# Cached keys of the samples turned by VectorE in squares of 32x32 instead of by TensorE

## The chip, the core and the metric

The kernel runs on one core of one Trainium2 chip. The time is the device time of one execution in microseconds; the kernel before takes 1926.86 us, the median of three runs (1926.57 to 1928.02).

## What is computed

One step of a layer of a streaming encoder, for a prompt (1024 frames) and for 8 samples of 16 new frames each, with shared weights and float32 throughout. The parts that the change touches, for the samples:

```python
k_all = concat([cache_fox_k, k], axis=1)      # 512 cached + 16 new rows, 8 heads x 64
s = einsum('bqhd,bkhd->bhqk', q, k_all) * 64 ** -0.5 + cq - ck    # branch A, causal
p = softmax(s); o = einsum('bhqk,bkhd->bqhd', p, v_all)
s = einsum('bqhd,bmhd->bhqm', qm, cache_mem_k) * 128 ** -0.5      # branch C, 256 rows, 4 heads x 128
```

Around it lie the input projection, the same attentions for the prompt, a pooling branch, gates and an output projection, and a feed-forward layer with 4096 inner channels.

## The kernel before

Every float32 product is made of parts: an operand is split into a high part (rounded to the fast format by a ScalarE copy) and a low part (the rest, by a VectorE subtraction), and TensorE multiplies high by high, high by low and low by high (`COMBOS`). A weight is so loaded by SP (`load_weights`, L570), its high part made on ScalarE (`split_hi`, L579) and its low part on VectorE (`split_lo`, L597), two buffers deep.

The order of the work is written out by hand. `plan` is the list of projection steps (weights of 128 columns over the tokens in blocks of 384); `product` (L1654) runs half a block, 12 matmuls of 128x384 (in `br` steps, with half the weights, a whole block). The attentions are cut into pieces, and the dictionary `beside` (built by `put`) says in front of which half block each piece is issued; every engine walks the same list and issues its own share of each piece, then the step's own evictions (`leave`) and, at a step's first half, the split of the next weight. So the pieces of the samples stand between half blocks of products on TensorE, in order on each engine.

Branch A's samples are worked in the halves of the steps `qm` and the first `gate` of branch 1, branch C's samples later beside `gate` and `br` steps of branch 1. Each sample i has three pieces, `sample(k, 3 * i + part)`:

- part 0: TensorE multiplies the queries, laid out in `qpad` with zeros for the other heads, by the turned keys `kt`, four quarters of 128 channels one after the other, each waiting for its `kt_lo` (`scores`, L1407); then the values of sample i - 1 (`values`, L1424, L1430). VectorE adds the bias and takes the maximum (L2512), ScalarE exponentiates and scales (L1913, L1923), VectorE copies the output of i - 1 (L2483).
- part 1: TensorE turns the probabilities (`turn`, L1454) and the output of i - 1 (`turned_out`, L1441), then turns quarters 0 and 1 of the keys of i + 1 (`turn_keys`, L1374) into two PSUM banks. ScalarE makes the high parts of the probabilities, of these keys (`keys_hi`, L1882), of the values of i (L1943). VectorE makes the low parts of the probabilities (L2538, L2541) and of the keys (`keys_lo`, L2438), and copies the queries of i + 1 into `qpad` (`queries`, L2452).
- part 2: TensorE turns quarters 2 and 3 of the keys; ScalarE and VectorE make their parts, VectorE then the low part of the values (L2559, in two halves for branch A).

SP issues all loads in the same order: keys of i + 2 in part 2 (part 1 for branch C) once the keys of i + 1 are turned (`load_keys`, L815), then values, bias and the weights. Branch A has one key buffer behind the first sample's own (`kraw_first`, loaded in `fox`, L835), branch C two. `first` is the piece that prepares sample 0: keys, cleared `qpad`, queries. The new queries and keys of the samples (`QS`, `KS`) are written at the eviction of the projections q and k (`leave`), high part by ScalarE, low part by VectorE; GpSimd copies a sample's new keys behind its cached ones (L1133). GpSimd and VectorE also share the new rows' values (L1143 to L1147 on GpSimd). `refill` brings back the prompt's outputs (L2567) in the same halves.

## Time and profile before

| | |
|---|---|
| three runs | 1926.57, 1926.86, 1928.02 us |
| profiled execution, first to last instruction | 1926.4 us |
| its own time beside the span | not given apart; the runs' median is 0.5 us above the span |
| TensorE busy, weight loads busy | 1903.4 us (99%), 1869.4 us (97%) |
| VectorE, ScalarE, GpSimd busy | 1222.8, 842.7, 516.6 us |
| mean granted TensorE clock | 0.999 |
| branch A's samples, branch C's samples | about 545 to 660 us, 777 to 855 us |

Busy time of TensorE counts overlapping matmuls once; a matmul's duration there is longer than the distance between two starts, so costs on TensorE are read from starts.

### The profile page before, as it was taken

The page shows a single profiled execution, that of the slowest core. Times are in us where ns is not written, and L with a number is a line of the kernel's source. Part 1 is how long each engine was busy: PE and PEld are TensorE (multiplying, and loading weights), DVE is VectorE, ACT ScalarE, POOL GpSimd, SP SyncE. Part 2 cuts the span into 40 slices and gives each one's busy share as a digit, 9 for nine tenths or more (in the row PEclk, how much of TensorE's full clock was granted, in tenths as well). Part 3 has the DMA queues.
Part 4 walks back from the last instruction along what each step waited for, and adds up shares of the span by engine and source line. Part 5 has one row for each costly group of instructions (what it writes and reads, how often), then busy time and mean ns, then how long its engine had stood idle before and what let it go on. Part 6 is the DMA issues. An engine that isn't in the chain of part 4 may idle for free. (4 is left out here: it accounts for less than half of the span.)

```text
span 1926.4 us, 33099 instructions
## 1 busy us (share of the span) xinstructions
PE 1903.4 (99%) x12655; PEld 1869.4 (97%) x12655; DVE 1222.8 (63%) x2293; ACT 842.7 (44%) x1672; POOL 516.6 (27%) x547
## 2 busy tenths in 40 slices
PE   9999999999999999999999999999999999999998
PEld 8999999999999999999999999999999999999997
DVE  6685545454557666554334467687777977777765
ACT  7454434353546544443223332344444544444445
POOL 1004324250612123000000004276544433333320
PEclk9999999999999999999999999999999999999999
DMA  6451312213266643444233222233333433333323
GB/s 197 114 134 50 94 47 66 83 35 94 55 231 206 203 137 99 146 154 131 64 104 93 70 88 72 94 100 91 122 89 92 123 91 88 88 88 88 89 93 99
DMA packets 243601, 202.40 MB, mean 105 GB/s; under 512 B 16750, under 2 KB 217966, under 8 KB 243317
## 3 DMA queue, kind: packets, MB, share of 16 engines
q1 hardware_dynamic: 243445, 200.29, 34.8%
q8 instruction: 101, 1.65, 0.4%
q14 instruction: 55, 0.45, 0.1%
HBM read 166.62 MB, written 33.64 MB: 104 GB/s over the span
## 5 line engine op out<-in xcount | busy, mean ns | idle before, releaser
L1654 PE MATMUL ps<-act_hi,w_hi 128*128 128x384 f32 x1128 | 386.9, 343 | 0.9 <-DVE w_lo L597 0.6
L1654 PE MATMUL ps<-act_hi,w_lo 128*128 128x384 f32 x1128 | 378.0, 335 | 0.0
L1654 PE MATMUL ps<-act_lo,w_hi 128*128 128x384 f32 x1128 | 377.6, 335 | 0.0
L597 DVE TENSOR_TENSOR w_lo<-w_raw,w_hi 128x512 fp32r<-128x512 f32 (+1 forms) x200 | 198.0, 990 | 122.3 <-ACT w_hi L579 121.7
L1638 PE MATMUL ps<-ffs_hi,w_hi 128*128 128x288 f32 x832 | 245.8, 295 | 1.0 <-DVE h L2646 0.6
L1638 PE MATMUL ps<-ffs_hi,w_lo 128*128 128x288 f32 x832 | 245.2, 295 | 0.0
L1638 PE MATMUL ps<-ffs_lo,w_hi 128*128 128x288 f32 x832 | 244.9, 294 | 0.0
L1623 PE MATMUL ps<-bp_hi,pw_hi 128*128 128x288 f32 x784 | 231.6, 295 | 0.2 <-DVE pw_lo L2601 0.2
L1623 PE MATMUL ps<-bp_lo,pw_hi 128*128 128x288 f32 x784 | 231.3, 295 | 0.0
L1623 PE MATMUL ps<-bp_hi,pw_lo 128*128 128x288 f32 x784 | 231.2, 295 | 0.0
L579 ACT ACTIVATE w_hi<-w_raw 128x512 fp32r<-128x512 f32 (+1 forms) x200 | 152.6, 763 | 164.5 <-PE ps L1638 119.4
L1654 PEld LDWEIGHTS ps<-act_hi,w_hi 128*128 128x128 f32 x1128 | 212.2, 188 | 2.0 <-DVE w_lo L597 0.9
L1654 PEld LDWEIGHTS ps<-act_lo,w_hi 128*128 128x128 f32 x1128 | 212.2, 188 | 0.4
L1654 PEld LDWEIGHTS ps<-act_hi,w_lo 128*128 128x128 f32 x1128 | 211.7, 188 | 0.0
L1638 PEld LDWEIGHTS ps<-ffs_hi,w_hi 128*128 128x128 f32 x832 | 156.1, 188 | 2.1 <-DVE h L2646 1.4
L1638 PEld LDWEIGHTS ps<-ffs_hi,w_lo 128*128 128x128 f32 x832 | 156.1, 188 | 0.0
L1638 PEld LDWEIGHTS ps<-ffs_lo,w_hi 128*128 128x128 f32 x832 | 156.1, 188 | 0.0
L1623 PEld LDWEIGHTS ps<-bp_hi,pw_hi 128*128 128x128 f32 x784 | 147.0, 187 | 0.9 <-DVE pw_lo L2601 0.8
L1623 PEld LDWEIGHTS ps<-bp_hi,pw_lo 128*128 128x128 f32 x784 | 147.5, 188 | 0.0
L1623 PEld LDWEIGHTS ps<-bp_lo,pw_hi 128*128 128x128 f32 x784 | 147.2, 188 | 0.0
L1170 POOL TENSOR_TENSOR quad<-quad 128x576 f32<-128x576 f32 x16 | 26.3, 1654 | 412.5 <-DVE bp_lo L2595 412.3
L1117 POOL TENSOR_SCALAR fox_p<-fox_p,small 128x128 f32<-128x128 f32 (+7 forms) x64 | 110.6, 1728 | 92.9 <-DVE small L2359 91.3
(356 smaller groups left out, 4190.7 us busy)
## 6 DMA issues: line engine op xcount, KB each, us to landing
w_raw<-in_w_down_dram SPq DMA_DIRECT2D x112, 256.0 KB, 3.4
pair_raw<-in_w_up_dram SPq DMA_DIRECT2D x28, 1024.0 KB, 5.5
w_raw<-in_w_in_dram SPq DMA_DIRECT2D x44, 512.0 KB, 4.4
merged<-prod SPq DMA_DIRECT2D x48, 192.0 KB, 2.0
prev<-merged SPq DMA_DIRECT2D x48, 192.0 KB, 3.8
foxs_vraw<-in_cache_fox_v_dram SPq DMA_DIRECT2D x8, 1024.0 KB, 6.1
foxs_kraw<-in_cache_fox_k_dram SPq DMA_DIRECT2D x7, 1024.0 KB, 5.6
x_in<-in_x_prompt_dram SPq DMA_DIRECT2D x8, 512.0 KB, 4.5
```

Of the source, the lines that this page charges most:

```text
L579: nc.scalar.activation(W[c % 2][0][:, 0:kt, :], w_raw[c % 2][:, 0:kt, :], ACT.Copy).then_inc(w_hi, 1)
L597: nc.vector.tensor_tensor(W[c % 2][1][:, 0:kt, :], w_raw[c % 2][:, 0:kt, :], W[c % 2][0][:, 0:kt, :].bitcast(F32), ALU.subtract).then_inc( ...
L1117: nc.gpsimd.tensor_scalar(p, p, col(RC, u), None, ALU.mult).then_inc(at_s["p_ready"], 1)
L1170: last = nc.gpsimd.tensor_tensor(out, a, b, op)
L1623: last = nc.tensor.matmul(p_bank(q), PW[q % 4][a][:, t, :], BP[PART_ORDER[0].index(i)][z][:, t, :], start=(t == 0 and n == 0), stop=(t == ...
L1638: last = nc.tensor.matmul(bank(b)[:, 0:TQ], W[c % 2][a][:, t, :], FS[k % 2][z][:, t, TQ * h:TQ * (h + 1)], start=(t == 0 and m == 0), stop ...
L1654: last = nc.tensor.matmul(bank(b)[:, 0:width], W[k][a][:, t, :], moving[z][:, t, j * width:(j + 1) * width], start=(t == 0 and n == 0), st ...
```

## The change

The cached keys are no longer turned by TensorE. They are loaded so that VectorE's transpose, which turns each square of 32 partitions by 32 columns where it stands, gives the turned keys: rows of 32 keys go to 32 partitions, and each quarter of the 512 columns to its own group of 32 partitions, by four DMAs with runs of 128 columns (512 bytes) in place of one with runs of 512 (2 KB). Partition 32y + a of quarter j then holds channel 128y + 32j + a, and the queries are laid out alike, by copies of 32 partitions. Turned keys lie in a new buffer `kt_raw` in SBUF, from which ScalarE and VectorE take the two parts.

```diff
+            def send_keys(a, i):
+                for y in range(4):
+                    sp.dma_start(raw_keys(a, i)[quadrant(y), :, :], a.kd[i][:, :, y * P:(y + 1) * P]).then_inc(sa["k_in"], 16)
-                sp.dma_start(raw_keys(a, i)[:], a.kd[i]).then_inc(sa["k_in"], 16)
+                send_keys(a, i)
...
-                sp.dma_start(mqs_raw[:], mem_q[:, :, SEQ:T]).then_inc(me["in"], 16)
+                for h in range(MH):
+                    sp.dma_start(mqs_raw[quadrant(h), :, :],
+                                 mem_q[:, h, SEQ:T].rearrange("(j r) q -> r j q", r=QUAD)).then_inc(me["in"], 16)
...
+            reached(pool, "new_lo", 2)
...
-            def turn_keys(a, i, part):
...
-                    for t in range(a.tiles):
-                        last = nc.tensor.transpose(ps[:, j % 2, t * P:(t + 1) * P], raw[:, t, j * P:(j + 1) * P], ident[:])
-                    last.then_inc(sa["kt_over"], 1)
...
-                    if i + 1 < NB:
-                        turn_keys(a, i + 1, 0)
-                elif i + 1 < NB:
-                    turn_keys(a, i + 1, 1)
...
-                    nc.scalar.activation(a.b["kt"][0][:, j, 0:a.tiles * P], ps[:, j % 2, 0:a.tiles * P],
+                    nc.scalar.activation(a.b["kt"][0][:, j, 0:a.tiles * P], a.b["kt_raw"][:, j, 0:a.tiles * P],
...
+                    if args == (0, 0):
+                        for part, raw in ((QS, qs_raw), (KS, ks_raw)):
+                            nc.scalar.activation(part[0][:], raw[:], ACT.Copy).then_inc(st["new_hi"].sem, 1)
...
-                        last = nc.scalar.activation(rest[0][:, s.i, :], src[:, LAST:TB], ACT.Copy, scale=scale)
+                        for y in range(4):
+                            last = nc.scalar.activation(rest[quadrant(s.i), y, :], src[quadrant(y), LAST:TB],
+                                                        ACT.Copy, scale=scale)
...
+            def keys_turned(a, i, part):
+                c = a.base + i
+                if part == 0:
+                    dve.wait_ge(sa["k_in"], 64 * (c + 1))
+                    if i:
+                        dve.wait_ge(sa["s_over"], c)
+                for j in (2 * part, 2 * part + 1):
+                    nc.vector.transpose(a.b["kt_raw"][:, j, 0:a.tiles * P],
+                                        raw_keys(a, i)[:, :, quadrant(j)]).then_inc(sa["kt_over"], 1)
...
-                    nc.vector.tensor_tensor(a.b["kt"][1][:, j, 0:a.tiles * P], ps[:, j % 2, 0:a.tiles * P],
+                    nc.vector.tensor_tensor(a.b["kt"][1][:, j, 0:a.tiles * P], a.b["kt_raw"][:, j, 0:a.tiles * P],
...
             def queries(a, i):
...
                 for x in range(2):
-                    w = P + NQ * per
-                    z, side = (x, 0) if a.new else (0, P // 2 * x)
-                    for h in range(per):
-                        r = slice(P // per * h, P // per * (h + 1))
-                        dst = a.b["qpad"][z][r, :].rearrange("p (j w) -> p j w", w=w)[:, :, side + h * NQ:side + (h + 1) * NQ]
-                        last = nc.vector.tensor_copy(dst, a.q[x][r, :, i * NQ:(i + 1) * NQ].bitcast(F32))
+                    for y in range(4):
+                        at_ = a.b["qpad"][x if a.new else 0][quadrant(y), :]
+                        new = a.q[x][quadrant(y), :, i * NQ:(i + 1) * NQ].bitcast(F32)
...
+                    keys_turned(a, 0, 0)
+                    keys_turned(a, 0, 1)
                     keys_lo(a, 0, 0)
+                    if a.new:
+                        for n, (part, raw) in enumerate(((QS, qs_raw), (KS, ks_raw))):
+                            reached(dve, "new_hi", n + 1)
+                            nc.vector.tensor_tensor(part[1][:], raw[:], part[0][:].bitcast(F32),
+                                                    ALU.subtract).then_inc(st["new_lo"].sem, 1)
...
                 elif part == 1:
+                    if i + 1 < NB:
+                        keys_turned(a, i + 1, 0)
                     dve.wait_ge(sa["pt_hi"], c + 1)
...
                 elif part == 2:
+                    if i + 1 < NB:
+                        keys_turned(a, i + 1, 1)
                     if i and a.new and i + 1 < NB:
                         out_lo()
-                    if i + 1 < NB:
-                        keys_lo(a, i + 1, 1)
                     dve.wait_ge(sa["v_hi"], c + 1)
...
                     for g in range(pieces):
...
+                        if g == 0 and i + 1 < NB:
+                            keys_lo(a, i + 1, 1)
...
-                    if j == 2:
-                        last = nc.vector.scalar_tensor_tensor(out=rest[1][:, s.i, :], in0=src[:, LAST:TB], scalar=scale,
```

`quadrant(y)` is the slice of partitions 32y to 32y + 31. `load_keys` waits as before for `kt_over`, which VectorE's transposes now count up.

## Rows read from the trace of the kernel before

**Rows 1.** The page: busy time, share of the span, instructions.

```profile
PE 1903.4 (99%) x12655; PEld 1869.4 (97%) x12655; DVE 1222.8 (63%) x2293; ACT 842.7 (44%) x1672; POOL 516.6 (27%) x547
```

**Rows 2.** Stretches: length, busy of PE, PEld, DVE, ACT, POOL, PEclk, DMA, GB/s.

```profile
557.65:572.55 14.90, 14.06 (x99) 13.43 (x100) 8.30 (x19) 7.42 (x14) 1.58 (x3) 1.00 0.87 302
601.19:615.28 14.09, 14.09 (x105) 13.95 (x104) 11.26 (x24) 8.72 (x17) 2.99 (x5) 1.00 0.71 227
...
795.66:805.57 9.91, 9.91 (x64) 9.38 (x63) 4.66 (x15) 5.03 (x13) 0.00 (x0) 1.00 0.43 151
815.60:825.40 9.80, 9.80 (x63) 9.27 (x63) 7.28 (x21) 4.67 (x12) 0.00 (x0) 1.00 0.76 223
```

**Rows 3.** Line L1374, the key turns: ns min/median/max, first and last start.

```profile
L1374 PE MATMUL ps<-ident,foxs_kraw x112: 272/272/331, 559.0 to 648.3; 128*128 128x128 f32 x112
...
L1374 PE MATMUL ps<-ident,mems_kraw x64: 270/272/328, 777.5 to 848.9; 128*128 128x128 f32 x64
```

**Rows 4.** Timeline of PE around the first group: start, length, instruction.

```profile
545.00 0.34 PE L1654 MATMUL ps<-act_hi,w_lo 128*128 128x384 f32 x1
545.18 1.03 PE L1374 MATMUL ps<-ident,foxs_kraw_first 128*128 128x128 f32 x8
545.97 0.42 PE L1654 MATMUL ps<-act_hi,w_hi 128*128 128x384 f32 x1
546.23 0.34 PE L1654 MATMUL ps<-act_lo,w_hi 128*128 128x384 f32 x1
```

**Rows 5.** Timeline of PE, one cycle of branch A.

```profile
601.19 0.60 PE L1454 MATMUL ps<-ident,foxs_p 128*128 128x128 f32 x4
...
608.14 0.40 PE L1407 MATMUL ps<-foxs_kt_hi,foxs_qpad_hi 128*128 128x264 f32 x2
...
611.05 0.64 PE L1424 MATMUL ps<-foxs_v_hi,foxs_pt 128*128 128x256 f32 x4
...
615.28 0.60 PE L1454 MATMUL ps<-ident,foxs_p 128*128 128x128 f32 x4
```

**Rows 6.** Timeline of DVE, the same cycle.

```profile
601.39 1.23 DVE L597 TENSOR_TENSOR w_lo<-w_raw,w_hi 128x1024 fp32r<-128x1024 f32 x1 [1.15 <-ACT w_hi L579]
602.99 0.69 DVE L2538 TENSOR_TENSOR foxs_pt<-ps,foxs_pt 128x512 fp32r<-128x512 f32 x1 [0.37 <-ACT foxs_pt L1932]
...
604.19 1.29 DVE L2438 TENSOR_TENSOR foxs_kt_lo<-ps,foxs_kt_hi 128x512 fp32r<-128x512 f32 x2
...
605.87 0.39 DVE L2452 CAST foxs_qpad_hi<-qs_hi 64x64 fp32r<-64x64 f32 x2
...
606.70 0.23 DVE L2488 TENSOR_TENSOR branch_lo<-o_part,branch_hi 128x64 fp32r<-128x64 f32 x1
607.75 1.29 DVE L2438 TENSOR_TENSOR foxs_kt_lo<-ps,foxs_kt_hi 128x512 fp32r<-128x512 f32 x2 [0.82 <-ACT foxs_kt_hi L1882]
608.95 2.35 DVE L2559 TENSOR_TENSOR foxs_v_lo<-foxs_vraw,foxs_v_hi 128x1024 fp32r<-128x1024 f32 x2
```

**Rows 7.** Timeline of ACT, the weight's high part in that cycle.

```profile
600.32 1.04 ACT L579 ACTIVATE w_hi<-w_raw 128x1024 fp32r<-128x1024 f32 x1
```

**Rows 8.** Timeline of DVE in branch C, the copies of the queries.

```profile
798.11 0.18 DVE L2452 CAST mems_qpad_hi<-mqs_hi 128x64 fp32r<-128x64 f32 x1
798.21 0.19 DVE L2452 CAST mems_qpad_hi<-mqs_lo 128x64 fp32r<-128x64 f32 x1
```

**Rows 9.** The first key load on SP's queue; DMA issues: KB each, us to landing.

```profile
539.26 0.43 SPq L835 DMA_DIRECT2D foxs_kraw_first<-in_cache_fox_k_dram  x1
...
w_raw<-in_w_in_dram SPq DMA_DIRECT2D x44, 512.0 KB, 4.4
...
foxs_kraw<-in_cache_fox_k_dram SPq DMA_DIRECT2D x7, 1024.0 KB, 5.6
```

**Rows 10.** Timeline of PE: first scores of branch A and of branch C.

```profile
551.67 0.51 PE L1407 MATMUL ps<-foxs_kt_hi,foxs_qpad_hi 128*128 128x264 f32 x2 [0.39 <-DVE foxs_qpad_lo L2452]
...
782.56 0.28 PE L1407 MATMUL ps<-mems_kt_hi,mems_qpad_hi 128*128 128x256 f32 x1
```

More of the change, by code:

```diff
@@ L68, in encoder_program @@
     V_LO = 32
+    QUAD = 32
     NTOK = 5
@@ L398, in encoder_program @@
         MQS = parts("mqs", [P, BT, P], R_AT + 65536)
-        sm = dict(kraw=[tensor(f"mems_kraw{k}", [P, MT, 512], R_AT + 36864 * k) for k in range(2)], vraw=tensor("mems_vraw", [P, MT, 512], R_AT + 4096),
-                  kt=parts("mems_kt", [P, 4, MT * P], R_AT + 8192), v=parts("mems_v", [P, MT, 512], R_AT + 16384),
+        sm = dict(kraw=[tensor(f"mems_kraw{k}", [P, NMEM // QUAD, P], R_AT + 36864 * k) for k in range(2)], vraw=tensor("mems_vraw", [P, MT, 512], R_AT + 4096),
+                  kt=parts("mems_kt", [P, 4, MT * P], R_AT + 8192), kt_raw=tensor("mems_kt_raw", [P, 4, MT * P], R_AT + 8192 + 16 * MT * P), v=parts("mems_v", [P, MT, 512], R_AT + 16384),
                   p=tensor("mems_p", [P, MT * P], R_AT + 24576),
@@ L405, in encoder_program @@
                   os=tensor("mems_os", [P, 4, P], R_AT + 69632),
-                  qpad=parts("mems_qpad", [P, 4 * (P + NQ)], R_AT + 31744))
+                  qpad=parts("mems_qpad", [P, 4 * P], R_AT + 31744))
         gate1 = tensor("gate1", [P, T], R3_AT + 1536)
@@ L834, in fox @@
                     sp.wait_ge(at_s["s_over"], UNITS)
-                    sp.dma_start(raw_keys(samples[0], 0)[:], samples[0].kd[0]).then_inc(sa["k_in"], 16)
+                    send_keys(samples[0], 0)
                 if s == 18:
@@ L1359, in fox @@
                     turn(s - 2)
-            def turn_keys(a, i, part):
-                c = a.base + i
-                if part == 0:
-                    pe.wait_ge(sa["k_in"], 16 * (c + 1))
-                    if i == 0 and a.new:
-                        pe.wait_ge(at_s["s_read"], UNITS)
-                    elif i == 0:
-                        pe.wait_ge(at_s["exp"], UNITS + M_UNITS)
-                for j in (2 * part, 2 * part + 1):
-                    if 4 * c + j >= 2:
-                        pe.wait_ge(sa["kt_lo"], 4 * c + j - 1)
-                    raw = raw_keys(a, i)
-                    for t in range(a.tiles):
-                        last = nc.tensor.transpose(ps[:, j % 2, t * P:(t + 1) * P], raw[:, t, j * P:(j + 1) * P], ident[:])
-                    last.then_inc(sa["kt_over"], 1)
             def sample(k, s):
@@ L1547, in beside_pe @@
                     fox(*args)
-                elif what == "first":
-                    turn_keys(samples[args[0]], 0, args[1])
                 elif what == "sample":
@@ L2128, in leave @@
                 elif s.kind in ("q", "k"):
-                    dst, rest, scale = (fq, QS, FD ** -0.5) if s.kind == "q" else (fk, KS, 1.0)
+                    dst, rest, scale = (fq, qs_raw, FD ** -0.5) if s.kind == "q" else (fk, ks_raw, 1.0)
                     if s.i == 0 and s.kind == "q" and j == 0:
@@ L2442, in queries @@
             def queries(a, i):
-                c, per = a.base + i, a.heads // 4
+                c = a.base + i
                 if i:
```

31 lines of the change are left out of this document (21 added, 10 removed).

## The prediction

> **What bounds the kernel now.** I read the page first: TensorE is busy for 99% of the span [rows 1], so the first guess is that work taken from it is time won. Then the table of stretches, one row per cached sample: two cycles of branch A (forgetting attention over 512 cached keys, 8 samples) and two of branch C (256 memory keys, 8 samples). TensorE has no idle time in the middle cycles, and VectorE is busy for 11.26 of 14.09 us in the first kind, 7.28 of 9.80 us in the busiest of the second [rows 2]. So TensorE bounds both stages, but VectorE has only about 2.5 to 3 us per sample left, and this change puts work exactly there. All of it lies in 545 to 660 and 777 to 855 us; the rest of the span keeps its time.
>
> **What it removes.** TensorE turns 16 blocks of keys per sample in A (128 in all, 112 of them in the first row) and 8 per sample in C (64) [rows 3]. Their 272 ns are pipelined times. What they cost is read from the order of starts: products start 0.18 us apart (545.00, 545.18); a group of eight starts at 545.18, the products behind it at 545.97 and 546.23, so the group costs 546.23 - 545.18 - 0.17 = 0.88 us [rows 4]. 16 groups of eight in A are 14.1 us, 16 groups of four in C at half that 7.1 us: 21 us is the most that the removal can give.
>
> **What it adds, per sample of A.** Four VectorE turns of 128x512 from SBUF to SBUF. No row shows such an instruction. The nearest are the 128x512 subtractions: 1.29 us for two in a row [rows 6]. I take 1.29 us for a pair. Lower bound: nothing (a gain from it has no reason); upper: twice that, 2.6 us a pair, if four-byte squares go at half the rate. Second, the copies of the queries become eight of 32 partitions instead of four of 64. The 64x64 copies take 0.39 us for two that start 0.20 us apart [rows 6], the 128x64 copies of C start 0.10 us apart though each takes as long [rows 8]. Copies that change their partitions do not overlap. So I take 0.20 us each: 1.6 us instead of 0.8 in A, 1.6 instead of 0.2 in C; if they did overlap, 0.8 in both. The Trainium skill ("VectorE: DVE Perf Modes", section on two Vector instructions with no wait between them) says that an instruction is held until all earlier ones have finished when its start quadrant of 32 partitions differs from the last one's; all eight copies would be held, and the trace agrees. Had I read the 128x64 row alone, the sum below would be 10 us lower, and the rule gives the other reading. Subtractions and high parts now read SBUF instead of PSUM: 1.29 us for two against half of 2.35 us for two of twice the width [rows 6], no difference.
>
> **The path of one cycle of A.** Take the cycle that begins when TensorE starts to turn the probabilities at 601.19. Before: turns, key turns, a product, key turns, a product, scores at 608.14, values at 611.05, a product, next cycle at 615.28, 14.09 us [rows 5]. The scores take 2.91 us, so the third quarter of the keys is read 1.46 us in, at 609.6; VectorE's low part of it, the first of the pair at 607.75, is ready at 608.4 [rows 6]: 1.2 us of slack, and that is why TensorE never waits.
> After: the pair of turns for quarters 1 and 2 stands ahead of the subtraction at 602.99 and falls into VectorE's idle time. Then as before up to 605.87; copies to 607.5; turns of quarters 3 and 4 to 608.8; the output's low part (0.25) 609.05; the first half of the value's low part, now moved ahead (half of 2.35 us), 610.2; low part of quarter 3 at 610.85, of quarter 4 at 611.45 [rows 6]. TensorE, rid of both groups, is at the scores at 608.14 - 1.76 = 606.4, waits for the queries until 607.5, reaches quarter 3 at 609.0 and waits until 610.85. Then 1.46 for two quarters and 4.23 for values and product [rows 5]: 616.5 against 615.28, +1.25 us. What VectorE has still to do between the low part of quarter 4 and the next probabilities is what it had, and stays within the 5 us that TensorE needs from there. Six cycles: +7.5 us.
> In three of these VectorE also has a weight's low part (1.23 us, after ScalarE's high part of 1.04 us [rows 6, 7]). Today both lie in the gap before 602.99. In the new order the turns stand behind them: 1.04 + 1.15 + 1.29 = 3.5 us after the cycle's start instead of 1.8, some +1.55 each: +4.65 us.
> The cycle from the first to the second sample took 14.90 us [rows 2], for waits of its own; by the same path, without the output parts (0.7), it takes 14.6: -0.3.
> **The first sample.** The keys were issued at 539.26 [rows 9]; four issues end some 1.3 us later, so the last part lands at about 546.2 (5.6 us [rows 9]). From there VectorE: four turns 2.5, two subtractions 1.25, two new ones for the new queries and keys 1.25, two clears, reckoned like subtractions, 1.2, two subtractions 1.25, copies 1.6: 555.3, where the scores started at 551.67 [rows 10]: +3.6 us. TensorE's saved 1.76 us are inside it.
> **Sum for A:** 3.6 - 0.3 + 7.5 + 4.65 = +15.45 us.
>
> **C.** Turns are half as wide (0.32 us each), keys are double buffered. At the start four turns (1.3) and longer copies (1.4) come ahead of the scores that started at 782.56 [rows 10]; I put some 1.6 of these 2.7 us into VectorE's waits: +1.1. In cycles like 815.60 to 825.40 VectorE has 7.28 + 1.3 + 1.2 = 9.8 us of work in 9.8 [rows 2], the gate products' evictions stand in its path, and each gets some 0.6 longer (three of seven); in quiet ones like 795.66 (4.66 busy [rows 2]) TensorE waits 0.6 us of the 0.88 saved plus what it waited for anyway, -0.4 (two); two stay as they are. Sum +2.1 us.
>
> **Parts costed at nothing.** In the projections ScalarE gets three more small copies in eight evictions and VectorE loses one: the bank is needed again two blocks of 4.2 us later; without that cover some 0.8 us each, 6 us. Four key loads instead of one are three issues of 0.4 us more on SP, ahead of values and weights that are asked for a cycle before use. The four loads of the memory queries lie before branch C. GpSimd's new wait is for parts made well before its copies of the new keys, behind which only its value copies queue.
>
> **Total:** 15.45 + 2.1 = +17.6 us on the profiled execution's 1926.4 us of span: 1944.0 us. The three runs' median, 1926.86 us, stands 0.5 us above that span; I leave this within the rounding. 0.2%, about what a measurement tells from no change, is 3.9 us. The bounds of my own case: copies that overlap take 0.8 from each of 15 cycles (-10); turns at 1 us more a pair add some 12: 1934 to 1956.
>
> **Rivals.**
> *VectorE swallows it and TensorE's saving shows (faster).* For it: 99% [rows 1], and that the first pair of turns lies in idle time. Against: the 1.2 us of slack in quarter 3's path. If turns cost nothing and copies start 0.10 apart, quarter 3 is ready at 608.75 and the cycle ends at 614.45: -0.85 in six, -1.8 in the first cycle, +0.3 at the start, -6.5 in C: -13, 1913 us. It decides only where a pair of turns takes under about 0.4 us; with copies 0.20 apart even free turns give no more than 1923.
> *Squares at half rate.* Another 1.29 us for each pair: six cycles +7.2, weights' cycles +3.6, start and first cycle +3.6, C +6: 1964 us. For it: nothing in the trace; against: every row's time goes with its elements.
> *The keys come late.* The load of sample i+2 now waits for VectorE's turns (608.8) instead of TensorE's (606), and its turns are wanted by 617.0 at the latest: 8.2 us, against 5.6 for rows of 2 KB and 4.4 for half the bytes in rows of 512 B [rows 9], so between 5.6 and 8.8. Twice 4.4 costs 0.6 a cycle. If it is 10.5 us: 2.3 in six cycles and 3.6 at the start, +17: 1961 us. The Trainium skill ("SBUF — State Buffer", section Door 1) has a rule against this part of the change: a transfer to 32 partitions reaches 8 of 16 ports, 189 GB/s instead of 328 at 1 MiB; by it the load takes an estimated 2.3 us more, 7.9, and nothing is lost. No run here shows such a load yet.
>
> **How the numbers follow.** Forecast 0.68 (of it 0.08 within 0.2% of before, if copies overlap and turns are at 0.4 us), faster 0.12 (the rows' slack speaks against it, but I never saw a turn), half rate 0.09, late keys 0.11. The range 1923 to 1962 leaves out nearly the whole of the faster case and half of the half-rate one, under 2 in 10. Faster 0.12, same 0.08, slower 0.80.
>
> **What would show it.** Right: no turns on TensorE, A's cycles of 15 to 17 us, TensorE waiting within the scores for the low key parts and for the query copies, turns of 0.6 to 0.7 us, copies 0.20 apart. Wrong: A's cycles at 12.4 us and no waits before the scores, turns of 0.3 us; or long waits of VectorE for the key load, or turns over 1 us.

## The result and the profile after

The changed kernel takes 1965.78 us (median of four runs, 1963.82 to 1968.43) against 1927.0 us (1926.57 to 1928.02) for the kernel before: ratio 1.0201, interval [1.0189, 1.0214]. Forecast were 1944 us and a range to 1962. The profiled execution has a span of 1961.9 us, 35.5 more than before's 1926.4; the forecast for that span was +17.6. Below, the table of stretches is read against spans, and runs against medians.

The page of the changed kernel, first part, answers to [rows 1]: TensorE 5.0 us less, VectorE 47.2 us more.

```profile
PE 1898.4 (97%) x12463; PEld 1862.4 (95%) x12463; DVE 1270.0 (65%) x2431; ACT 853.6 (44%) x1698; POOL 520.3 (27%) x547
```

The table of stretches of the changed kernel (length, busy of PE, PEld, DVE, ACT, POOL, PEclk, DMA, GB/s): up to the first sample's turn, the first cycle, the third, the last; it answers to [rows 2].

```profile
540.00:564.24 24.24, 17.27 (x94) 16.60 (x92) 14.09 (x34) 7.06 (x14) 3.32 (x7) 0.86 0.86 215
564.24:580.75 16.51, 12.66 (x83) 11.80 (x83) 10.64 (x26) 7.51 (x14) 0.00 (x0) 1.00 0.94 233
601.28:620.38 19.10, 14.89 (x88) 14.56 (x87) 14.63 (x32) 10.34 (x18) 3.71 (x5) 0.82 0.64 161
674.92:692.00 17.08, 14.06 (x89) 13.71 (x88) 11.88 (x29) 8.84 (x17) 3.66 (x5) 0.90 0.34 102
```

A cycle here is the time from one sample's first turn of probabilities to the next sample's. Cycles of branch A take 16.5 to 20.5 us instead of 14.1 to 14.9, and the granted clock, 1.00 throughout before, is 0.82 to 0.90 in six of the seven. By places: the first turn of probabilities stands at 564.24 instead of 557.65 (+6.6), the last at 692.00 instead of 657.66 (+34.3), the first scores of C at 815.85 instead of 782.56 (+33.3), the end at +35.5. So nearly all of the loss is in A.

TensorE's timeline in the third cycle of the changed kernel answers to [rows 5] (those rows are of the fourth cycle; there the changed kernel waits 3.28 us before the scores and takes 17.34 us in all). The scores wait 4.21 us, for the previous output's low part (`branch_lo`), and then start 0.44 us apart, two at a time, where they started 0.24 apart before (last two lines, kernel before).

```profile
610.80 0.78 PE L1406 MATMUL ps<-foxs_kt_hi,foxs_qpad_hi 128*128 128x264 f32 x2 [4.21 <-DVE branch_lo L2507]
611.38 0.64 PE L1406 MATMUL ps<-foxs_kt_lo,foxs_qpad_hi 128*128 128x264 f32 x2
611.82 0.64 PE L1406 MATMUL ps<-foxs_kt_hi,foxs_qpad_lo 128*128 128x264 f32 x2
```

```profile
608.38 0.40 PE L1407 MATMUL ps<-foxs_kt_lo,foxs_qpad_hi 128*128 128x264 f32 x2
608.62 0.40 PE L1407 MATMUL ps<-foxs_kt_hi,foxs_qpad_lo 128*128 128x264 f32 x2
```

VectorE's timeline in the same cycle, and GpSimd's beside it, answer to [rows 6]:

```profile
600.76 1.30 DVE L2439 STREAM_TRANSPOSE foxs_kt_raw<-foxs_kraw 128x512 f32<-128x512 f32 x2 [0.69 <-DMA foxs_kraw<-in_cache_fox_k_dram]
...
604.34 1.71 DVE L2446 TENSOR_TENSOR foxs_kt_lo<-foxs_kt_raw,foxs_kt_hi 128x512 fp32r<-128x512 f32 x2
605.97 0.45 DVE L2515 TENSOR_TENSOR o_part<-ps,o_part 64x64 f32<-64x64 f32 x2
606.45 1.85 DVE L2460 CAST foxs_qpad_hi<-qs_hi 32x64 fp32r<-32x64 f32 x4
608.31 0.79 DVE L2460 CAST foxs_qpad_lo<-qs_lo 32x64 fp32r<-32x64 f32 x4
609.13 1.30 DVE L2439 STREAM_TRANSPOSE foxs_kt_raw<-foxs_kraw 128x512 f32<-128x512 f32 x2
610.36 0.18 DVE L2507 TENSOR_TENSOR branch_lo<-o_part,branch_hi 128x64 fp32r<-128x64 f32 x1
```

```profile
604.41 1.09 POOL L1158 CAST foxs_vnh<-foxs_vnraw 16x512 fp32r<-16x512 f32 x1 [13.63 <-DMA foxs_vnraw<-out_dram]
605.56 0.95 POOL L1160 CAST foxs_vn<-foxs_vnraw 16x512 fp32r<-16x512 f32 x1
606.59 1.25 POOL L1162 TENSOR_TENSOR foxs_vn<-foxs_vnraw,foxs_vnh 16x512 fp32r<-16x512 f32 x1
```

Turns are as forecast (1.30 us a pair), copies too where nothing holds them (0.79 for four). But two low parts take 1.71 instead of 1.29 and the first four copies 1.85 instead of 0.8, both while GpSimd works on the new values. GpSimd starts on them 3.1 us after the cycle's first turn here and 6.4 us after it in the second cycle; before it was 1.9 to 3.4 us, so only the second cycle is clearly late (GpSimd's long wait for their load is there before, too: 10 us and more).

### The profile page after: what moved, and what is told of

Same layout as the page of the kernel before. It is cut to its first block and busy times, and to the rows that moved or that the text cites. A ratio compares the mean times of both kernels' runs of the same rounds, so it can differ in the third digit from the quotient of the medians.

```text
span 1961.9 us, 32929 instructions
## 1 busy us (share of the span) xinstructions
PE 1898.4 (97%) x12463; PEld 1862.4 (95%) x12463; DVE 1270.0 (65%) x2431; ACT 853.6 (44%) x1698; POOL 520.3 (27%) x547
```

## The experiments

Each has the kernel before beside it on the same chip; ratios are to that. What a run "gives back" is the difference of its median to the changed kernel's 1965.78 us, measured at another time; the medians of the kernel before lay between 1926.3 and 1927.7 us. First the order of VectorE's queue.

**1.** In part 2, the output's low part, for which the scores wait, goes ahead of the turns of quarters 3 and 4.

```diff
+                    if i and a.new and i + 1 < NB:
+                        out_lo()
                     if i + 1 < NB:
                         keys_turned(a, i + 1, 1)
-                    if i and a.new and i + 1 < NB:
-                        out_lo()
```

> The changed kernel with one line moved: in part 2 VectorE makes the output's low part (which TensorE's scores of branch A wait for) before, not after, the turns of quarters 3 and 4. VectorE's total work is the same. Theory (VectorE's path sets the end of the scores, and the long single wait before them costs a second time because TensorE's granted clock is halved after it): the wait of 3.0 to 4.3 us before the scores becomes 1.7 to 3.0, with a second wait of about 2 us for the low part of quarter 3 inside them; if two shorter waits keep the clock up, the branch's mean clock rises from 0.82-0.90 to near 1.00 and the time falls by 8 to 18 us from 1965.8; the path alone would give 0 to 2. Rival 'late keys': no change, the loads start as before. Rival 'path alone, the clock is no cost of its own': within 2 us of 1965.8.

1963.25 us, 1.0190 [1.0173, 1.0207]: 2.5 us, within the two intervals, so nothing like the 8 to 18 us of the expectation. From the third sample on the waits before the scores are still 2.65 to 5.66 us: the query copies end just ahead.

**2.** All four turns at the start of part 1.

```diff
                     if i + 1 < NB:
                         keys_turned(a, i + 1, 0)
+                        keys_turned(a, i + 1, 1)
...
-                    if i + 1 < NB:
-                        keys_turned(a, i + 1, 1)
```

> The changed kernel with all four turns of a sample's keys at the start of part 1, in VectorE's idle time before the probabilities' high part, instead of two there and two in part 2. Theory: part 2's path gets 1.3 us shorter, part 1's longer by 0 to 1.3 us (the idle time there is 1.1 us beside 1.3 of turns, none with a weight); the wait before the scores shrinks from 3.0-4.3 to 2-3.5 us, and the key loads start 7 us earlier: 1950 to 1962, depending on the clock. Rival 'late keys': VectorE's waits for the loads (0.7 and 1.1 us in two cycles) go, and with them the whole loss, to 1935 or less. Rival 'path alone, conserved': 1962 to 1968.

1952.97 us, 1.0135 [1.0119, 1.0150]: 12.8 us back, the largest single piece. Half the turns stood on the path to the scores, and could stand in front of the probabilities' low part. The run changes more than the path, though. The line holds for branch C too: in the traces A gets 8.9 us shorter, and 2.1 come from behind it. The copies of the queries' high part now mostly miss GpSimd's work (206 ns on average instead of 311), and VectorE waits for keys of samples 2 to 8 for 0.5 us in all instead of 1.8. How the 8.9 us divide among these was not tested.

**3.** As 2, and the scores wait for `o_sum` instead of `o_done`.

> All four turns at the start of the piece (as in the run that measured 1952.97 us), and in branch A the scores wait for the sum of the previous output's parts (o_sum), which is all that reads their bank, instead of for the output's low part (o_done), which VectorE makes last. Theory (the low part only stands at the end of the same VectorE queue; the query copies end 0.2 to 0.5 us before it and the scores wait for those then): 1949 to 1952 us, waits of 1.5 us and more before the scores remain and their releaser becomes the query copies. Rival (the wait for the low part is the cost of its own): waits under 0.5 us, clock 1.00, 1935 to 1942 us.

1953.44 us, 1.0143 [1.0128, 1.0158], no gain over run 2: TensorE's waits are now put down to the query copies, as the theory had it.

```profile
611.11 0.51 PE L1406 MATMUL ps<-foxs_kt_hi,foxs_qpad_hi 128*128 128x264 f32 x2 [1.72 <-DVE foxs_qpad_lo L2460]
```

**4.** As 3, with the query copies of samples 1 to 7 made by ScalarE in part 0.

> As e5_o_sum, with the eight query copies of samples 1 to 7 of branch A made by ScalarE, in its idle time behind the scaling of the probabilities. Theory (what delays the scores is VectorE's row of work ahead of them, the copies with what GpSimd does to them its largest part): waits before the scores fall below 1 us in most samples, the clock of 564 to 680 us is at 0.97 or above, cycles of 12.4 to 14 us, 1936 to 1944 us. Rival (it is the low parts of quarters 3 and 4 or the values' high part on ScalarE that are late, waits come back within the scores): 1946 to 1952 us. Slower than e5_o_sum if ScalarE's small copies delay the high parts of weight and probabilities: over 1953 us.

1956.51 us, 1.0157 [1.0142, 1.0172]: 3.1 us slower than run 3. Eight copies take ScalarE 2.1 us, a weight's high part stands behind them, and in three of the six samples the scores then wait for GpSimd's copies of the new keys, queued behind the new values, in the other three for `o_part` (TensorE's timeline, then ScalarE's):

```profile
607.84 0.78 PE L1406 MATMUL ps<-foxs_kt_hi,foxs_qpad_hi 128*128 128x264 f32 x2 [3.96 <-POOL foxs_kt_lo L1148]
```

```profile
616.11 1.03 ACT L1926 ACTIVATE foxs_qpad_hi<-qs_hi 32x64 fp32r<-32x64 f32 x4
617.15 1.05 ACT L1926 ACTIVATE foxs_qpad_lo<-qs_lo 32x64 fp32r<-32x64 f32 x4
```

**5.** The best order I could find, all work kept: turns and copies of sample i+1 in part 0 of i, `o_sum`, GpSimd's new keys ahead of its new values.

```diff
+                if part == 0 and i + 1 < NB and a.new:
+                    queries(a, i + 1, (0,))
                 if part == 0 and i < NB:
                     dve.wait_ge(sa["exp"], c + 1)
...
+                if part == 0 and i + 1 < NB and a.new:
+                    queries(a, i + 1, (1,))
+                    keys_turned(a, i + 1, 0)
+                    keys_turned(a, i + 1, 1)
```

> The change in another order, all of its work kept: in branch A VectorE makes the four turns and the query copies of sample i+1 in part 0 of sample i (copies of the high part while it waits for the exponential, turns behind the copy of the previous output, ahead of the next weight's low part), the scores wait for the outputs' sum, and GpSimd copies the new keys of i+1 ahead of the new values of i. Theory (the order of VectorE's queue, GpSimd's and the clock that follows from the waits make up the loss beside the loads): waits before the scores under 1 us from the third sample on, clock of 600 to 700 us at 0.97 or above, 1932 to 1941 us; what stays is the first sample (6 us) and the loads (9 us). Rival (VectorE's sum of work per sample, about 13 us with what GpSimd adds, is what bounds the stage, whatever its order): cycles of 13.5 to 15 us, 1941 to 1950 us. Third (with the order mended the key loads, whose issue waits for the turns, become the wait): VectorE waits 1 to 2 us for kraw in every cycle, 1942 us or more.

1952.64 us, 1.0128 [1.0111, 1.0145]. The forecast for this run missed, and its rival too, by less. VectorE is busy for 37.74 of 40 us (third number behind the length), so the rival "its sum bounds the stage" fits from 620 us on; in the second cycle it waits 3.74 us for keys, 6.8 us in four cycles, where the third said 1 to 2 us in every cycle (a stretch; VectorE's timeline).

```profile
620.00:660.00 40.00, 32.76 (x213) 31.55 (x211) 37.74 (x78) 24.84 (x46) 12.37 (x13) 0.96 0.67 171
```

```profile
587.14 2.49 DVE L2445 STREAM_TRANSPOSE foxs_kt_raw<-foxs_kraw 128x512 f32<-128x512 f32 x4 [3.74 <-DMA foxs_kraw<-in_cache_fox_k_dram]
```

Second, the loads, in all three kernels.

**6.** The kernel before with the new loads alone, TensorE turning (the keys' order so differs from the reference's).

```diff
+            def send_keys(a, i):
+                for y in range(4):
+                    r = slice(32 * y, 32 * y + 32)
+                    sp.dma_start(raw_keys(a, i)[r, :, :].rearrange("p t (u c) -> p (t u) c", c=P), a.kd[i][:, :, y * P:(y + 1) * P]).then_inc(sa["k_in"], 16)
...
-                sp.dma_start(raw_keys(a, i)[:], a.kd[i]).then_inc(sa["k_in"], 16)
+                send_keys(a, i)
```

> The kernel before with the new key loads alone: four DMAs to 32 partitions each with runs of 512 bytes in place of one with runs of 2 KB; TensorE turns what lies there, so that the keys are in another order than the reference's. Theory: the loads have 9 to 10 us before TensorE wants them, landing gets 1 to 3 us later at most: 1926 to 1929. Rival 'late keys': TensorE waits for the loads, 1932 or more.

1935.70 us, 1.0046 [1.0031, 1.0061]: 8.7 us, against an expectation of at most 2. TensorE waits for both of the first loads, and the first turn of probabilities comes 4.0 us late; the second cycle takes another 4.4 us more than before:

```profile
547.61 1.29 PE L1380 MATMUL ps<-ident,foxs_kraw_first 128*128 128x128 f32 x8 [2.56 <-DMA foxs_kraw_first<-in_cache_fox_k_dram]
```

**7.** The changed kernel with the old loads (the keys' order differs as in run 6).

> The changed kernel with its key loads as before: one DMA per sample in runs of 2 KB over 128 partitions (the keys so turned are not those of the reference; instructions on the engines are the same in number and size). Theory (the loads cost 8.7 us in the kernel before, where TensorE waited for them at the first two samples, and the same must go here): 1954 to 1959 us, VectorE's waits for kraw gone, first turn of probabilities at 561 to 563 instead of 564.2. Rival (in the changed kernel VectorE's order of work is late anyway and hides the loads): 1962 to 1966 us. Third (the loads also start the falls of the clock): under 1953 us.

1956.40 us, 1.0155 [1.0138, 1.0172]: 9.4 us back.

**8.** Run 5 with the old loads (again in another order).

> As f1_reordered, with the key loads as before (one DMA per sample in runs of 2 KB; the keys so turned are not the reference's). Theory (loads cost 8 to 9 us wherever VectorE or TensorE is near the path): 8 to 10 us below f1_reordered, 1923 to 1932 us, so at most level with the kernel before. Rival (they only cost at the first two samples, 2 to 4 us): 1930 us or more. If the saving of 12 to 21 us on TensorE is to be had at all, this run is under 1920 us.

1943.37 us, 1.0080 [1.0065, 1.0095]: 9.3 us below run 5, as expected, but still over the kernel before; the 1923 to 1932 us that went with it did not come.

Third, GpSimd.

**9.** The three `nc.gpsimd` operations on the new values cut from `[low, :]` and `[0:NQ, :]` to `[low, 0:NQ]` and `[0:NQ, 0:NQ]` (the other new values are left out).

> The changed kernel with GpSimd's three operations on the new values of a sample cut from 512 columns to 16 (the other new values' columns are left at zero). Theory (GpSimd's and VectorE's work on SBUF hold each other: query copies of 1.1 to 2.2 us for four instead of 0.8, key low parts 1.71 instead of 1.29; some 0.5 to 1.5 us per cycle on the path to the scores): 1955 to 1961 us, every four copies 0.78 us, two low parts 1.29. Rival (their overlap does not lie on the path): 1962 to 1966 us.

1956.95 us, 1.0159 [1.0144, 1.0174]: 8.8 us back. VectorE's groups of 562 to 700 us, changed kernel and then this run (count | busy, mean ns): the hold (GpSimd's work keeping VectorE's waiting, and the other way round) is gone from low parts and copies.

```profile
L2446 DVE TENSOR_TENSOR foxs_kt_lo<-foxs_kt_raw,foxs_kt_hi 128x512 fp32r<-128x512 f32 x28 | 20.7, 780 | 0.2
...
L2460 DVE CAST foxs_qpad_hi<-qs_hi 32x64 fp32r<-32x64 f32 x28 | 8.7, 311 | 0.5
```

```profile
L2446 DVE TENSOR_TENSOR foxs_kt_lo<-foxs_kt_raw,foxs_kt_hi 128x512 fp32r<-128x512 f32 x28 | 18.1, 689 | 0.2
L2460 DVE CAST foxs_qpad_hi<-qs_hi 32x64 fp32r<-32x64 f32 x28 | 5.3, 189 | 0.5
```

The copies were held in the kernel before as well, though: their high parts average 365 ns there in the same window, where the copies of the low part, of the same size, take 189. So the run takes away more than the change added.

```profile
L2452 DVE CAST foxs_qpad_hi<-qs_hi 64x64 fp32r<-64x64 f32 x14 | 5.1, 365 | 0.3
```

Fourth, TensorE's freed time and its clock.

**10.** The changed kernel with 24 transposes of the identity on TensorE ahead of every sample's scores in A.

> The changed kernel with 24 transposes of the identity (128x128, into a PSUM bank that nobody reads) on TensorE in front of every sample's wait for the scores in branch A: some 2.6 us of work at full clock where it waits 3 to 6.6 us today. Nothing else changes, VectorE's path least of all. Theory (clock is a cost of its own): clock 0.98 to 1.00 in branch A, scores of 2.9 us instead of 4.5 to 5.1, cycles of about 16 us instead of 18, time 1947 to 1956. Rival 'path alone': 1964 to 1968, as the filler can only fill waits. Rival 'late keys': the same as path alone.

1959.51 us, 1.0171 [1.0156, 1.0187]: 6.3 us back, for 24 instructions more per sample; less than I expected. The granted clock of 564 to 700 us is 0.96 instead of 0.89. The third cycle below has a clock of 1.00, TensorE still waits 1.58 us in it before the scores, and it takes 16.87 us: there VectorE's row sets the pace.

```profile
597.98:614.85 16.87, 15.29 (x112) 14.96 (x111) 14.75 (x31) 9.60 (x18) 3.61 (x5) 1.00 0.62 154
```

**11.** The changed kernel with TensorE's 16 turns per sample given back as dead work.

```diff
+                if a.new and part and i + 1 < NB:
+                    for n in range(8):
+                        nc.tensor.transpose(ps[:, n // 4, n % 4 * P:(n % 4 + 1) * P], ident[:], ident[:])
```

> The changed kernel with TensorE's work given back and nothing else: 16 transposes of 128x128 of the identity per sample of branch A (8 behind part 1, 8 behind part 2, for seven samples), with no waits and no readers. If TensorE's saving reached the end of the stage, this costs 7 times 1.76 us: 1978 us. Theory (TensorE waits for VectorE by more than 1.76 us per sample, so the saving was worth nothing, and the transposes also shorten the waits that let the clock fall): 1957 to 1966 us.

1962.31 us, 1.0182 [1.0167, 1.0197]. TensorE's saving, the whole point on which 12 us hung, is worth nothing here; without it the kernel is no slower. (The dead work also shortens the waits that the clock falls in, so this is the sum of both.)

**12.** Both: 16 given back, 28 ahead of the scores.

> The changed kernel with TensorE's turns given back (16 transposes of the identity per sample) and 28 more ahead of every sample's scores in branch A, so that TensorE hardly rests. If the low clock is a cost of its own beyond what VectorE sets: clock 1.00 in 565 to 700 us and 1952 to 1957 us, below the run with 24 transposes (1959.51 us, clock 0.96). If VectorE's queue alone sets the cycle once the clock is above 0.95: 1957 to 1961 us at a clock of 1.00. Over 1962 us if the transposes themselves now stand in the way.

1962.26 us, 1.0174 [1.0157, 1.0192], which is the expectation's third case: the transposes themselves stand in the way. In the third cycle (first line) TensorE is busy for all of its 17.13 us and does not wait before the scores, as in the second and the fifth, so these cycles say nothing of VectorE. In the fourth, with a weight (second line), TensorE waits 0.26 us for `branch_lo` and VectorE's row is as full: it is busy for 15.96 of 17.73 us, against 11.26 of 14.09 in the same cycle before [rows 2]. Its timeline shows from one copy of the previous output to the next (613.17 to 631.31) two waits only, both for ScalarE.

```profile
597.49:614.62 17.13, 17.13 (x133) 17.01 (x131) 14.63 (x31) 9.98 (x18) 3.00 (x5) 1.00 0.65 160
614.62:632.35 17.73, 17.47 (x132) 17.11 (x131) 15.96 (x33) 9.28 (x17) 3.25 (x5) 1.00 0.73 185
```

```profile
613.17 0.69 DVE L2510 COPY foxs_om<-ps 128x512 f32<-128x512 f32 x1
615.01 1.23 DVE L601 TENSOR_TENSOR w_lo<-w_raw,w_hi 128x1024 fp32r<-128x1024 f32 x1 [1.15 <-ACT w_hi L583]
...
631.23 0.16 DVE L2556 RECIPROCAL small<-small 128x1 f32<-128x1 f32 x1 [0.90 <-ACT foxs_p L1914]
631.31 0.69 DVE L2510 COPY foxs_om<-ps 128x512 f32<-128x512 f32 x1
```

In A this trace is 7.0 us shorter than the changed kernel's (last turn at 685.03), at the end only 1.7. The rest lies outside A. The stretch from A's last turn to C's first is 2.2 us longer, and two of C's cycles take 12.66 us at a granted clock of 0.87 instead of 11.1 at 1.00 (this run, then the changed kernel, the fourth cycle of C):

```profile
844.50:857.16 12.66, 10.92 (x54) 10.17 (x55) 10.54 (x33) 4.82 (x12) 0.00 (x0) 0.87 0.75 206
```

```profile
849.33:860.43 11.10, 9.36 (x54) 8.63 (x54) 10.18 (x33) 4.82 (x12) 0.00 (x0) 1.00 0.71 202
```

Such cycles stand in the traces of runs 1, 5, 7, 8, 17 and 18 too, one in each, though A was all that most of these edits touched. So a trace's end tells less of A than its last turn does, and a step of 3 us between two runs can come from behind A.

**13.** Run 5 with the 24 transposes.

> As f1_reordered, with 24 transposes of the identity on TensorE ahead of every sample's scores in branch A. Theory (the waits left are short and do not lower the clock): the 24 transposes cost their 2.6 us per sample where TensorE is not waiting, so 1940 to 1955 us, slower than f1_reordered. Rival (the clock still falls in f1_reordered): 4 us or more below f1_reordered.

1948.93 us, 1.0111 [1.0096, 1.0127]: the clock is 1.00 from 580 us on, and the run is 3.7 us faster instead of slower, so even there TensorE had waits to fill; the expectation had this the other way round.

Fifth, VectorE's share.

**14.** The kernel before, with four dead turns into the low parts' place and eight query copies of 32 partitions for samples 1 to 7; TensorE turns the keys.

```diff
+                    for j in (2 * part, 2 * part + 1):
+                        nc.vector.transpose(kt_dead[:, j, 0:a.tiles * P], ...)
```

> The kernel before, in which TensorE still turns the keys and loads are as they were, with VectorE's share of the change added for samples 1 to 7 of branch A as dead work: four turns of 128x512 per sample into the place of the low parts, two ahead of the probabilities' low part and two ahead of the output's, and eight query copies instead of four. Theory (the loss is VectorE's work and its place in the queue, with the waits and the falls of the clock that follow; the loads are the other 9 us and the first sample some 4): 1945 to 1957 us, waits of 2 us and more before the scores, granted clock under 0.95 in 580 to 660 us. Rival (the reading of the path alone, 1.25 + 1.76 us per cycle at most since TensorE arrives later): 1930 to 1942 us, clock 1.00.

1939.85 us, 1.0065 [1.0050, 1.0080]: +12.7 us. The rival's time fits, and nearly its clock: from the third sample on the waits before the scores are 0.85 to 2.27 us, and the clock is 0.91 in the second cycle, with the longest wait, and 1.00 in the others. From first to last turn of probabilities it takes 113.3 us instead of 100.0; 5.0 of the 13.3 us fall in that second cycle.

```profile
590.98:606.23 15.25, 14.40 (x105) 13.83 (x103) 11.96 (x30) 9.25 (x18) 2.91 (x5) 1.00 0.49 146
606.23:622.86 16.63, 14.75 (x104) 13.84 (x104) 14.54 (x33) 9.45 (x17) 2.91 (x5) 1.00 0.68 207
```

**15.** The same with the new loads.

> g4_vector_share_alone (1939.85 us) with the new loads added (four DMAs per sample in runs of 512 bytes; the keys so turned are in another order than the reference's), TensorE still turning the keys. If the two costs add: 1939.85 + 8.7 = 1948 to 1950 us, and the rest up to the changed kernel's 1965.8 is the first sample's longer row on VectorE and what comes of TensorE's freed time (longer waits, lower clock). If they feed each other (late values and new rows make GpSimd's work fall on VectorE's, waits pass 3 us and the clock falls though TensorE keeps its turns): 1953 to 1962 us.

1945.81 us, 1.0094 [1.0079, 1.0109]: +6.0 more than run 14, where the loads alone cost 8.7: they don't feed each other.

**16.** The kernel before with the eight copies alone.

> The kernel before with eight query copies of 32 partitions instead of four of 64 for samples 1 to 7 of branch A, nothing else. Theory (the prediction's slack: the third quarter's low part is ready 1.2 us before it is read, the copies take 0.8 of it): 1926 to 1929 us, copies 0.20 us apart. Rival (there is no such slack since the output's low part, for which the scores wait, stands behind the copies): 0.2 to 0.8 us in each of seven cycles, 1929 to 1933 us.

1930.05 us, 1.0015 [1.0006, 1.0024]: +2.9 us, in the rival's range, though the interval (1.2 to 4.6 us) reaches into the theory's. Two waits for `branch_lo` before the scores show, of 1.02 us at 580.10 and of 0.25 at 623.39.

**17.** The changed kernel with four copies of 64 partitions for samples 1 to 7 (`two = slice(QUAD * y, QUAD * (y + 2))`; half of the queries so lie in wrong columns).

> The changed kernel with the query copies of samples 1 to 7 of branch A cut from eight of 32 partitions to four of 64 (half of them so lie in wrong columns). Theory (VectorE's row of work ahead of the scores has no slack, so each 0.2 us taken out comes back in full, plus what GpSimd's hold adds, plus some clock): 4 to 9 us below the changed kernel, 1957 to 1962 us. Rival (the copies lie in the shadow of ScalarE's high part of the output, for which the low part waits): 1964 to 1967 us.

1959.44 us, 1.0171 [1.0155, 1.0187]: 6.3 us back, or 0.9 per sample for 0.8 us of work, which fits a row without slack. It is weak evidence: the four executions lie between 1957.10 and 1963.47 us, and in the trace, of the slowest, branch A is only 2.0 us shorter.

**18.** Run 8 with GpSimd's operations cut and four copies: of the change, only turns and TensorE's saving remain in A.

> f1_reordered (1952.64 us) with the old loads, GpSimd's value operations cut to 16 columns and four query copies instead of eight: of the change only VectorE's turns and TensorE's saving are left in branch A. Theory (VectorE's sum per sample bounds the stage; it is now 15.0 - 0.8 of copies - 0.4 to 1.0 of GpSimd's hold = 13.2 to 13.8 us): cycles of 13.2 to 14.2 us, 1930 to 1936 us. Rival (once all that surrounds the turns is gone, TensorE's 1.76 us per sample shows): cycles of 12.4 to 12.8 us, 1918 to 1925 us.

1936.19 us, 1.0045 [1.0028, 1.0062]. Cycles of 13.4 and 14.5 us at a clock of 1.00, VectorE busy for 12.26 and 13.39 of them, against 14.1 before: a gain of 0.2 us per cycle (98.7 us for the seven instead of 100.0), 5.2 us lost ahead of the first and 5.0 behind A, of these 3.7 in C's cycles.

```profile
605.93:620.44 14.51, 12.83 (x89) 12.25 (x88) 13.39 (x28) 9.57 (x17) 2.84 (x5) 1.00 0.74 241
620.44:633.80 13.36, 12.83 (x88) 12.24 (x88) 12.26 (x27) 9.46 (x18) 1.90 (x5) 1.00 0.62 190
```

No version beat the kernel before.

**The ledger**, from runs that lead from one kernel to the other, in medians (the intervals reach some 2 to 3 us to either side, so the last step is not clear of them):

| step | us |
|---|---|
| kernel before | 1927.0 |
| VectorE's share, samples 1 to 7 of A (run 14) | +12.8 |
| the new loads (15) | +6.0 |
| keys really turned by VectorE: first sample, low parts out of SBUF beside GpSimd, turns waiting for loads, branch C (11) | +16.5 |
| TensorE's turns taken away (the change) | +3.5 |
| the changed kernel | 1965.8 |

By places in the traces of runs 15 and 11 the third row divides into 3.2 us ahead of the first turn of probabilities, 8.4 in A's seven cycles and 4.1 behind A.

## Why the prediction was wrong

**What held.** The side, and half of the mechanism: VectorE's row of work makes the scores wait. Where they wait is not what the path said, see below. Two rivals are out: no saving shows, and squares don't go at half rate (0.65 us a turn in a pair). Copies stand 0.20 us apart. The path of one cycle was forecast at +11.85 us over the seven cycles (7.5 + 4.65 - 0.3); VectorE's share alone, run 14, gives +13.3. That the two are near is luck: in run 14 TensorE keeps its turns, the value's low part stays behind the keys', 5.0 us fall in one cycle, and the waits stand before the scores. Branch C was forecast at +2.1 us (1.1 at its start, 1.0 in its cycles); from A's last turn to C's first scores the trace has -1.0, from there to the end +2.2, so +1.2 in all, with waits of 1.50 to 1.75 us in four samples and 0.20 in two. One trace can't settle so small a term: between A and C the changed runs spread from -1.3 to +1.8 us.

```profile
815.85 0.39 PE L1406 MATMUL ps<-mems_kt_hi,mems_qpad_hi 128*128 128x256 f32 x1 [1.50 <-DVE mems_qpad_hi L2464]
826.29 0.39 PE L1406 MATMUL ps<-mems_kt_hi,mems_qpad_hi 128*128 128x256 f32 x1 [1.55 <-DVE mems_kt_lo L2446]
835.87 0.39 PE L1406 MATMUL ps<-mems_kt_hi,mems_qpad_hi 128*128 128x256 f32 x1 [0.20 <-DVE mems_kt_lo L2446]
```

**The steps that failed**, against 18.9 us missing in A (34.3 - 15.45), 3.0 of them ahead of the first turn. The path gave a cycle 15.3 us, with a weight 16.9; the trace has 17.1 to 19.1 and 17.3 to 20.5 (the weight's extra, forecast at 1.55, is about 1.1 on average). Its first cycle was to take 14.6 us and took 16.5.

*"Parts costed at nothing", the loads.* 6 to 9 us (runs 6, 7, 8, 15). Only the three more issues were looked at and found early enough for loads "asked for a cycle before use". At the first two samples no such lead exists, and what stands behind the key loads lands later: the 1 MB of values takes 7.4 us instead of 6.1 (median of the page's DMA issues). The rival of late keys had the cause right, but at 17 us instead of 9, and most of it in six cycles where VectorE hardly waits for keys: it does so for 1.17 us at the first sample and for 1.8 in two cycles. From the first issue (539.21) to VectorE's first turn the load took 7.9 us (timelines of SP and of VectorE, changed kernel):

```profile
539.21 2.09 SPq L815 DMA_DIRECT2D foxs_kraw_first<-in_cache_fox_k_dram  x4
```

```profile
547.07 2.49 DVE L2439 STREAM_TRANSPOSE foxs_kt_raw<-foxs_kraw_first 128x512 f32<-128x512 f32 x4 [1.17 <-DMA foxs_kraw_first<-in_cache_fox_k_dram]
```

From the rates in the Trainium skill ("SBUF — State Buffer", section Door 1) the prediction had worked out an estimated 7.9 us for such a load. The trace's time is the same, but no run tells what the 32 partitions cost in it from the 2.09 us that the four issues take. The conclusion drawn from the estimate, that nothing is lost below 8.2 us, was mine and wrong: it priced one load, not the queue behind it.

*"Subtractions ... now read SBUF instead of PSUM: ... no difference."* True alone, not beside GpSimd. With PSUM as one input the low parts average 686 ns although GpSimd has all its work (the group of run 14, below) and some of it at the same moment (610.65 to 611.94); with two SBUF inputs 780, which is (780 - 686) x 28 = 2.6 us. The copies of the queries' high part cost (311 - 189) x 28 = 3.4 us of hold, but in the kernel before already (365 - 189) x 14 = 2.5. So the change added some 3.6 us of hold on VectorE, and the 8.8 us that taking GpSimd's work away gave (run 9) are an upper bound of its part.

```profile
L2448 DVE TENSOR_TENSOR foxs_kt_lo<-ps,foxs_kt_hi 128x512 fp32r<-128x512 f32 x26 | 16.7, 686 | 0.4
```

The Trainium skill has the rule ("SBUF — State Buffer", section "SBUF: two separate sides"): VectorE and GpSimd share one pair of ports, which an operation of VectorE with two SBUF inputs holds against a GpSimd operation that reads SBUF, whichever comes first, the other waiting it out. The trace agrees for the low parts (and GpSimd's cast takes 1.09 us beside them at 604.41, alone 0.61), and shows the same for the copies. It should have been a term of the sum, since the change turns a PSUM input into an SBUF one.

*"The path of one cycle": what releases the scores.* The sum let them start at the copies' end, at 607.5, and wait within them for the third quarter's low part. In the trace that second wait stands in one sample only (1.28 us at 573.19); from the third sample on all of the waiting is before the scores. They also wait for the output's low part (`o_done`), which the change puts behind the turns of quarters 3 and 4: 1.3 us more ahead of the scores, overlooked. By itself this is worth little (run 1, 2.5 us): the query copies in the same row end nearly as late. Turning all quarters early gives 12.8 us back (run 2, with what else it moves), so half of the turns had been put where they cost most. (`kt_raw` lies in the low parts' place, so no turn can start before the scores of the sample ahead are done.)

*"The path of one cycle": the clock, not in it at all.* In the changed kernel TensorE waits 3.0 to 6.7 us before the scores from the third sample on, and the granted clock of their cycles averages 0.82 to 0.90, which mixes stretches at 1.2 and at 2.4 GHz. Behind the wait of 4.21 us the scores ran at 0.51, so at 1.2 GHz, and took 5.36 us instead of 2.91 (the changed kernel, then the kernel before):

```profile
610.80:616.16 5.36, 5.36 (x24) 5.36 (x25) 4.44 (x6) 1.85 (x3) 0.00 (x0) 0.51 0.95 174
```

```profile
608.14:611.05 2.91, 2.91 (x25) 2.91 (x25) 2.91 (x4) 1.00 (x2) 0.00 (x0) 1.00 0.85 255
```

For the first sample, scores to first turn take 564.24 - 555.78 = 8.46 us instead of 557.65 - 551.67 = 5.98: 2.5 of the 3.0 us that the start missed; its VectorE row, forecast to end at 555.3, ended at 555.7. Over the seven cycles the runs with the clock raised or held (10, 12) are 4.9 and 6.3 us shorter in the trace (122.8 and 121.4 against 127.8); in the runs' time they gave 6.3 and 3.5 us. Run 12 understates it, since its transposes fill TensorE. VectorE's row sets most of the pace either way: run 10's third cycle takes 16.87 us at a clock of 1.00.

These prices overlap: removed one at a time from the changed kernel, loads 9.4, GpSimd 8.8, order 12.8, copies 6.3 and clock 6.3 add up to 43.6 us, more than the whole loss of 38.8, since each shortens the same waits. How the 16.5 us of the third row of the ledger divide by cause stays open. (One slip in the prediction's own bounds: 0.8 us from each of 15 cycles is 12 us, not 10.)

**TensorE's saving.** I put it at 21 us at most. Run 18, with all but the turns taken away, gains 0.2 us per cycle of the 1.76 saved. With VectorE at 12.3 to 13.4 us of a 12.3 us budget of TensorE there was nothing more to win.

## What to carry to other kernels

Before moving work to an engine with slack, add its whole round per iteration: its busy time, the new work, and the waits inside the round that stay. Here 11.26 + 2.6 + 0.8 of work, 0.9 for the exponential and 1.15 for the weight make 16.7 us against TensorE's 12.3, before any hold by GpSimd; run 12 has 17.73 for that cycle. The sum is a lower bound: for the third cycle, without a weight, it gives 10.13 + 2.6 + 0.8 + 0.9 = 14.4 us, and run 10 has 16.87, with 1.5 of hold and 0.9 of waits for keys and probabilities. When an operand moves from PSUM to SBUF, look who else reads SBUF then. When one DMA becomes four, price what is queued behind it and the first iteration, where nothing is fetched ahead. And an engine whose saved work turns into a wait may also lose its clock: fill such a wait and see, before counting the saving.

## What the runs showed of the hardware that was not expected

VectorE turns 32x32 squares of float32 at the pace of a subtraction: 128x512 in 686 ns (median of 28), with input read in runs of 32 elements 512 bytes apart; in run 14, where the input lies in one piece, the average is 688. Loads in runs of 512 B to 32 partitions keep the DMA engines busier than loads in runs of 2 KB to 128, for the same data (no run changes the two apart): from 600 to 680 us the changed kernel shows a share of 0.64 at 164 GB/s, with the old loads (run 7) 0.48 at 154 (the last two numbers of each row):

```profile
600.00:680.00 80.00, 64.36 (x390) 62.85 (x388) 63.05 (x136) 42.30 (x76) 18.22 (x25) 0.87 0.64 164
```

```profile
600.00:680.00 80.00, 64.73 (x396) 63.07 (x395) 64.82 (x149) 42.85 (x77) 15.98 (x23) 0.89 0.48 154
```

And a kernel can be made faster by giving TensorE 24 transposes per sample that nobody reads (run 10, 6.3 us).
